# Hymba decode step: GpSimd multiplies every second page of decode keys, 16 of 32, where it took 12

## The reference

```python
def gather(c):
    g = c[i, page_table]
    return g.reshape((db, past_len) + g.shape[3:])
...
ka_all = jnp.concatenate([past_ka, ka], axis=1)
k_split = ka_all.reshape(b, s_len, H_A, 2, DH_A)
s1 = jnp.einsum('bqhd,bshd->bhqs', a1, k1).astype(jnp.float32) * scale
s2 = jnp.einsum('bqhd,bshd->bhqs', a2, k2).astype(jnp.float32) * scale
pr = jax.nn.softmax(s1, axis=-1) - lam * jax.nn.softmax(s2, axis=-1)
```

## Time and profile before

| what | us |
|---|---|
| median of three timed runs | 3538.22 |
| lowest and highest of them | 3528.4 and 3543.82 |
| the profiled execution | 3525.9 |
| its span, from first to last instruction | 3524.3 |

### The profile page before, as it was taken

How to read it: one execution, slowest core, us unless ns; L and a number is a source line. 1 busy time by engine, 2 the same in 40 slices (tenths; PEclk the granted TensorE clock), 3 DMA queues, 4 the chain that set the end, 5 groups by cost and what they waited for, 6 DMA issues and landing times. The chain is left out here.

```text
span 3524.3 us, 45823 instructions
## 1 busy us (share of the span) xinstructions
PE 3332.7 (95%) x17235; PEld 2281.7 (65%) x17265; DVE 1553.3 (44%) x2769; ACT 810.9 (23%) x1781; POOL 778.0 (22%) x992
## 2 busy tenths in 40 slices
PE   5878999999999999999999999999999998999999
PEld 3666777777777677777788888887444444444443
DVE  2025887878777787765434553112000023111111
ACT  4011233333425242433112222222100002000000
POOL 0005664646474655540000001000000000000000
PEclk8989999999999999999999999999999999999999
DMA  9866496878686877764301111103111023021010
GB/s 344 251 204 180 147 293 214 288 229 295 213 294 215 271 245 267 237 222 145 114 24 31 40 41 47 42 7 121 47 48 44 5 84 103 33 72 66 24 63 24
DMA packets 315102, 496.39 MB, mean 141 GB/s; under 512 B 26113, under 2 KB 211738, under 8 KB 313714
## 3 DMA queue, kind: packets, MB, share of 16 engines
q1 hardware_dynamic: 264512, 338.50, 30.1%
q0 software_dynamic: 46592, 146.84, 12.3%
q10 hardware_dynamic: 3778, 8.13, 0.6%
HBM read 466.02 MB, written 27.37 MB: 140 GB/s over the span
## 5 line engine op out<-in xcount | busy, mean ns | idle before, releaser
L1277 PE MATMUL Z<-W,hT 128*128 128x256 f32 x4608 | 1061.9, 385 | 16.7 <-DMA W<-in_w_in_dram 13.7
L1277 PEld LDWEIGHTS Z<-W,hT 128*128 128x128 f32 x4608 | 860.3, 191 | 173.8 <-issue 46.4
L2173 PE MATMUL S<-W,hT 128*128 128x512 f32 x1408 | 646.6, 597 | 1.8 <-SPq L2130 1.8
L2173 PEld LDWEIGHTS S<-W,hT 128*128 128x128 f32 x1408 | 265.1, 191 | 350.1 <-issue 347.3
L1588 PE MATMUL DB<-W,hT 128*128 128x256 f32 x1696 | 383.3, 381 | 0.0
L1588 PEld LDWEIGHTS DB<-W,hT 128*128 128x128 f32 x1696 | 316.3, 190 | 39.9
L996 DVE TENSOR_REDUCE sc<-big 128x16 f32<-128x1024 f32 x256 | 309.4, 1208 | 2.2 <-POOL big L816 1.7
L2173 PE MATMUL Z<-W,hT 128*128 128x512 f32 x640 | 303.6, 592 | 0.0
L992 DVE TENSOR_TENSOR big<-big,qb 128x1024 f32<-128x1024 f32 x160 | 231.8, 1449 | 76.4 <-DMA big<-in_cache_diff_k_dram 74.1
L816 POOL TENSOR_TENSOR big<-big,qb 128x1024 f32<-128x1024 f32 x96 | 231.3, 2410 | 101.9 <-DMA big<-in_cache_diff_k_dram 100.9
L2173 PEld LDWEIGHTS Z<-W,hT 128*128 128x128 f32 x640 | 121.5, 190 | 153.0 <-issue 152.6
(11 more groups left out here) (525 smaller groups left out, 3201.8 us busy)
## 6 DMA issues: line engine op xcount, KB each, us to landing
big<-in_cache_diff_k_dram POOLq DMA_DIRECT2D x256, 512.0 KB, 5.1
big<-in_cache_diff_v_dram SPq DMA_DIRECT2D x256, 512.0 KB, 4.6
W<-in_w_in_dram SPq DMA_DIRECT2D x27, 2048.0 KB, 9.9
W<-in_w_in_dram SPq DMA_DIRECT2D x52, 1024.0 KB, 8.1
W<-in_w_ple_gate_dram SPq DMA_DIRECT2D x16, 1024.0 KB
W<-in_w_out_dram SPq DMA_DIRECT2D x12, 1024.0 KB
kib<-in_cache_idx_k_dram POOLq DMA_DIRECT2D x256, 32.0 KB, 2.7
hT<-oT_d SPq DMA_DIRECT2D x3, 2048.0 KB, 20.4
```

The costliest lines, as they stand in the source:

```text
L1277: mm = pe.matmul(Z[b][:, 0:CW], hT[:, k, t * P:(t + 1) * P], W[:, w, k, :], start=(k == 0), stop=(k == KT - 1))
L2173: mm = pe.matmul(b, hT[:, k, t * P:(t + 1) * P], Wr[:, k, :], start=(k == 0), stop=(k == KT - 1))
```

## The change

The tuple of the pages that GpSimd multiplies is a different one: all odd pages (16 of 32), where it was pages 2, 5 and 7 of every eight (12 of 32). In slots 0 to 7 GpSimd's multiplies go from 96 to 128 and VectorE's from 160 to 128.

```diff
         SLOTS = HA + 1
-        POOL_PAGES = tuple(p for p in range(NPG) if p % 8 in (2, 5, 7))
+        POOL_PAGES = tuple(p for p in range(NPG) if p % 2)
         PAGES = {0: (3, 5, 5, 5, 4, 4, 3, 3)}
```

## The result

| what | before | after |
|---|---|---|
| median of six runs each, same chip, us | 3540.52 | 3558.24 |
| lowest and highest, us | 3528.4 and 3543.82 | 3552.86 and 3569.57 |
| the profiled execution, us | 3525.9 | 3561.2 |
| its span, us | 3524.3 | 3559.6 |

The ratio of after to before is estimated from all the runs at 1.0072, with a 95% interval from 1.0052 to 1.0091: the change makes the kernel about 0.7% slower. It is not the quotient of the two medians, which is 1.0050 (17.7 us); by either the change loses.

A forecast was written before the change was run, and what follows sets the result against it. TensorE, 95% busy, bounds it; its waits for VectorE's `combine` count, paced by GpSimd between tiles 1 and 4. 14.0 + 2.7 + 5.1 - 2.7 + 1.2 = +20.3 us on the 3538.2 median gives 3558.5; range 3523 to 3580.

The forecast's parts named there:

- the sum: Whole kernel: terms for tiles 4, 3 and 5, clock and slot 0 add to +20.3 us; bounds +7 to +38.
- the late slots: Slots 1, 4, 5 and 7 of the kernel before, taking 162.6 to 166.8 us where an undisturbed slot takes 160.1.
- GpSimd's term: Between tiles 1 and 4: two more multiplies, 4.7 us, less 1.2 earlier start; page 16's load issued 3.5 us later.
- Tile 4's distribution: TensorE's wait at tile 4: 3.5 us in each of four late slots (14.0), 2.7 us over the three others.
- slack: In slots not late, VectorE's `combine` of tile 4 ends 2.6 us before TensorE asks; taken off the 3.5 us.
- Tile 3: VectorE's multiply of page 10 ahead of `combine` makes TensorE wait 2.8 us, part of the 3.5 and not added.
- Tile 5: VectorE has one multiply fewer in tile 4's pages, so TensorE's waits at tile 5 shrink: -2.7 us, other bound 0.
- Clock: Longer TensorE waits lower the granted clock: three new drops at 1.7 us each, +5.1 us; bounds none and five drops.
- Slot 0: After the threshold work GpSimd's chain of loads starts behind VectorE's page 26: +1.2 us, bounds 0 and 4.7.
- rival 1: Exclusive stretch bounds everywhere: each moved page costs 1.13 us, 28 pages in slots 1 to 7, +32 us, 3570; chance 0.07.
- rival 2: Page landings set the pace and hide GpSimd's added work; only tile 5's -2.7 us remains, 3535.5; chance 0.22.
- rival 3: VectorE sets the pace and its relief pays: -15 us (3523), or -20 (3518) with slot 1's start; chance 0.13.

The follow-up runs named there:

- the run of the second half: Kernel before, with GpSimd multiplying the odd pages among 16 to 31 and the old ones (2, 5, 7, 10, 13, 15) below 16: 3530.0 us, ratio 0.9997.

## Why the prediction came out as it did

The direction, the forecast and its place were right: GpSimd paces the loads between tiles 1 and 4, page 16's load leaves later, TensorE waits for `combine`. The measured difference of the medians is 17.7 us, against the 20.3 of the sum. But part of that agreement is luck, and the step that carries the sum was wrong.

- *Which execution the sum is made against.* The two profiled executions differ by 35.3 us, not by 20.3. The sum was laid on a profiled execution that stood 12 us below the median of its kernel, and then moved up by those 12. After the change the profiled execution is 3 us above the median. Since the late slots of the pages' old placement are not the same from one kernel to another (the run of the second half), the execution that the sum was laid on, faster than all six timed ones, looks like a lucky one; with the change all slots are late in the one trace that there is. Between the two traces the sum is 15 us short.
- *GpSimd's term: the size was right, the cause was not.* Page 16's load leaves 3.5 us later on average, as worked out. But not because of two more multiplies at 2.354 us less 1.2: giving back one of them takes away all of the 3.5 (72.9), while seven of the eight stay. The sentence that failed is "Waits for a landing do not decide it: page 10's goes, and pages 3 and 11 get one instead". Page 3 waited 0.0 us in every one of slots 1 to 7; page 11 waited 2.8 to 5.1, where page 10 had waited 0.0 to 5.9 before, and its place, ahead of the reads and of page 14's load, is what counts. The average of 2.1 us that the sentence set against it is over all of a slot's waits, not over that stretch.
- *Tile 4's distribution.* Predicted: 3.5 us in each late slot, 0.9 in the three with slack. The load of page 16 does not move by a constant; in slots 2 to 7 it goes to between 75.3 and 77.4, from 70.4 to 76.2 before. So the slots that had been on time lose 6 to 9 us each, 23 together, where 2.7 was forecast; slots 1, 4, 5 and 7 lose 0.7, 4.7, 1.0 and 1.7, 8 together, where 14.0 was. The "slack" of 2.6 us did not absorb the move.
- *Tile 3.* The wait for page 10's landing between maxima and `combine` came, as said, but in slots 1, 2 and 6 alone, with 3.9, 1.2 and 6.2 us. Taking page 10 out of that place gains nothing certain (1.0055 against 1.0072, intervals that overlap).
- *Tile 5.* The sign was wrong: -2.7 predicted, and the waits there grew, in slot 4 from 0.67 to 2.18. Page 15's multiply is to page 18's load what page 11's is to page 14's (in slot 4 it waited 4.61 us), and page 18's load goes from 85.3 to 90.1. With 13.2 us in all, tile 5 has more of the waits than tile 3 or tile 4.
- *Clock.* 5.1 predicted, 7.1 measured as TensorE's longer busy time in slots 2 to 7.
- *Slot 0.* 1.2 predicted, with 4.7 as the upper bound. The wait at its end grew by 1.0 (5.4 to 6.4), which lies within the 3.5 to 7.3 of the other runs. But slot 1 starts 4.7 us later in the trace (421.0 against 416.3). Over the runs that start is at 412.8 to 413.9 in the four fastest and at 417.1 to 421.3 in those that lose, and also at 419.7 and 420.4 in two that do not (without page 11; the second half). So the term may have been too small by some 3 us; no run shows what sets it.

The rivals. *The exclusive stretch* (rival 1) would price page 11 at 1.13 us in each of eight slots, 9 us; it is worth 27 to 34. Single instructions are stalled: beside page 11's multiply L1122 took 2.01 us, and 0.22 in the run above where GpSimd stood still. That lengthens a `combine`, in slot 6 by 1.8 us and by 1.0 more in L1124, but it does not set the size. The Trainium skill, page "SBUF — State Buffer", section "Who interferes with whom", has VectorE and GpSimd share a port pair that one of them holds exclusively; the 2.01 us agree with it. *The landings absorb the work* (rival 2) fails with the pages of the change, and is near the truth where the multiply stands behind the reads and not right ahead of the load of page 10 or 14: 1, 5, 9 and 13 cost nothing. *VectorE is the pace* (rival 3) fails twice: four multiplies fewer per slot on VectorE are worth 0.2%, in an interval from 0.4% to none, and all 32 on VectorE are faster than before, 0.9925.

Open: what makes one slot late and the next one on time in the kernel before, with the same pages. Page 10's wait, 0.0 to 2.7 us in slots 2, 3 and 6 and 4.3 to 5.9 in slots 4, 5 and 7, goes with it, but no run sets it by itself. And the runs with none, four and eight pages on GpSimd (0.9925, 0.9913, 0.9932) are not told apart; any of them beats the kernel before by 0.7 to 0.9%, and the change by more.

## What to carry to other kernels

When an engine both computes and issues loads, price a moved instruction by the load that stands next behind it, not by its length: ask which load some other engine will wait for, and what is ahead of it in the queue, waits included. Place such work where the queue would have stood anyway (ahead of a wait for another engine, with other work between it and the load that it needs). Keep it out of the place right behind that load, and out of the place right ahead of a load that another engine will wait for: the run with 0, 1, 4, 5, 8, 9, 12 and 13 had almost no waits for landings and lost all the same. And before laying a sum on a profiled execution, see whether its stages are all alike: if some are late and some not with the same program, the trace is one draw of several.

## What the runs showed of the hardware

- Reading four page numbers into registers, where it stands behind a wait for GpSimd's own last piece, leaves GpSimd idle for 2.04 to 2.07 us ("issue" ahead of L793) in 55 of 62 places of the change and for 2.34 to 2.36 in the others. Reads added where no such wait stands ahead left it idle for 0.6 to 1.0 us, and in one place 1.3 more than before, and made nothing slower (0.9977).
- A load of one page of 512 KB landed 3.6 to 10.5 us after its issue in the change and 3.6 to 10.1 before (for the 128 of 256 loads whose landing the trace has). The median is 5.0 after and 5.1 before, so the change did not slow the transfers themselves.
- A tiny VectorE instruction that starts beside a GpSimd multiply of 128x1024 ended with it: of 14 such L1122 (128x1) in the change, 11 ended 0.01 to 0.03 us behind the multiply and three 0.35 to 0.52. The one of slot 6 took 2.01 us, where it takes 0.22 alone.
